# A three-block transformer kernel: compression weights in two transfers, the gate's weights in two ring slots, the first pair's sums on VectorE

## The reference, cut to what matters

```python
# first block
ssm = jax.nn.gelu(ssm)
ssm = ssm * jax.nn.sigmoid(ssm @ w_glu[l] + b_glu[l])      # w_glu: 512 x 512
x = x + _rms_norm(jnp.concatenate([attn, ssm], -1) @ w_out[l], post_norm_g[l])
# second block, for l in range(2)
parts = jnp.split(_rms_norm_2(x, g_pre_mix[l]) @ w_in[l], split_at, axis=-1)
hid = jax.nn.gelu(blocks @ w1 + b1)     # compression of keys, then of values: w1 is 2048 x 256
kc = hid @ w2 + b2                      # 31 blocks of 32 tokens, 2 heads: 62 columns
h = _rms_norm_2(x, g_pre_mlp[l])
y = jnp.square(jax.nn.relu(h @ w_up[l])) @ w_down[l]       # 1024 -> 4096 -> 1024
```

## Time and profile before

| | us |
|---|---|
| runs of the kernel before (median of 3) | 1707.92 |
| the profiled execution | 1710.8 |
| its span, first to last instruction | 1709.0 |
| TensorE busy | 1652.7 |
| VectorE, ScalarE, GpSimd busy | 1114.3, 713.3, 578.2 |

### The profile page before, as it was taken

The page is one execution under the profiler, slowest core; times in us unless marked ns, Lnnn a source line. Parts: engine busy times, 40 slices in busy tenths (PEclk is TensorE's granted clock), DMA queues, the critical chain, the costliest instruction groups (busy, mean ns, idle before and its releaser), DMA issues.

```text
span 1709.0 us, 25412 instructions
## 1 busy us (share of the span) xinstructions
PE 1652.7 (97%) x9539; PEld 1291.1 (76%) x9539; DVE 1114.3 (65%) x1955; ACT 713.3 (42%) x1426; POOL 578.2 (34%) x596
## 2 busy tenths in 40 slices
PE   7988999999999999999999999999999999999997
PEld 4455547478886668899889878887667888888886
DVE  6999756345337665777778655433774587778854
ACT  4233342252226654444444234233664454444322
POOL 1010001231205553544444724110564454444460
PEclk9999999998999999999999999899999999999999
DMA  6314230135311003333333313622000333333321
GB/s 195 68 25 93 56 123 1 28 99 165 93 50 63 2 1 99 96 102 100 99 99 99 102 37 104 184 69 99 14 2 1 99 111 100 99 99 100 100 97 49
DMA packets 195786, 137.68 MB, mean 81 GB/s; under 512 B 34871, under 2 KB 176946, under 8 KB 195666
## 3 DMA queue, kind: packets, MB, share of 16 engines
q1 hardware_dynamic: 189372, 128.86, 26.0%
q10 hardware_dynamic: 6294, 7.22, 1.8%
HBM read 131.00 MB, written 2.10 MB: 78 GB/s over the span
## 4 chain that ended last, share of the span: by engine, by line
PE 82%; DVE 9%; POOL 3%; issue 2%; DMA 2%; ACT 1%; ACTq 0%; SPq 0%; POOLq 0%; DVEq 0%
PE ps L564 14%; PE ps L565 14%; PE ps L566 14%; PE ps L2104 4%; PE ps L2105 4%; PE ps L2106 4%; PE ps L1984 4%; PE ps L2000 4%; PE ps L2015 3%; PE ps L1200 3%; PE ps L894 3%; PE ps L1879 1%; POOL U_LO L2700 1%; DMA WR<-in_cmp_w_v 1%; PE ps L1108 1%
## 5 line engine op out<-in xcount | busy, mean ns | idle before, releaser
L566 PE MATMUL ps<-HT_R,WR_R 128*128 128x512 f32 (+1 forms) x832 | 313.6, 377 | 0.0
L566 PEld LDWEIGHTS ps<-HT_R,WR_R 128*128 128x128 f32 x832 | 157.4, 189 | 32.1
L564 PE MATMUL ps<-HT_R,UP_HI 128*128 128x512 f32 x448 | 177.3, 396 | 0.0
L565 PE MATMUL ps<-HL_MLP,UP_HI 128*128 128x512 f32 x448 | 177.0, 395 | 0.0
L486 DVE TENSOR_TENSOR WR_R<-WR,UP_HI 128x1024 fp32r<-128x1024 f32 x56 | 99.9, 1785 | 103.2 <-ACT UP_HI L480 103.2
L2174 ACT ACTIVATE BIG<-ps 64x512 f32<-64x512 f32 (+3 forms) x124 | 71.7, 579 | 173.0 <-PE ps L566 153.4
L2502 DVE CUSTOM_DVE_ANT_0 ps<-ps,tri 128x512 f32<-128x512 f32 (+1 forms) x192 | 93.1, 503 | 57.8 <-PE ps L1984 57.1
L2674 POOL TENSOR_SCALAR BIG<-BIG,rg,gate 128x512 f32<-128x512 f32 (+3 forms) x128 | 76.3, 607 | 152.1 <-DVE rg L2518 151.8
L2274 ACT ACTIVATE BIG<-ps,mn 128x512 f32<-128x512 f32 (+1 forms) x192 | 100.2, 528 | 62.0 <-DVE mn L2502 54.0
L2700 POOL TENSOR_TENSOR U_LO<-BIG,U_HI 128x768 fp32r<-128x768 f32 (+1 forms) x48 | 120.5, 2531 | 1.9
L894 PE MATMUL ps<-WR,HT 128*128 128x512 f32 (+1 forms) x256 | 115.0, 600 | 1.2 <-ACT BIG L1677 1.2
(11 more groups left out here) (397 smaller groups left out, 4289.4 us busy)
## 6 DMA issues: line engine op xcount, KB each, us to landing
WR<-in_w_up SPq DMA_DIRECT2D x64, 512.0 KB, 4.0
WR<-in_w_down SPq DMA_DIRECT2D x96, 256.0 KB, 3.3
WR<-in_w_in SPq DMA_DIRECT2D x36, 512.0 KB, 5.3
WR<-in_w_out SPq DMA_DIRECT2D x6, 2048.0 KB, 7.9
WR<-in_w_in SPq DMA_DIRECT2D x5, 2048.0 KB, 8.2
WR<-in_w_down SPq DMA_DIRECT2D x16, 512.0 KB, 3.7
WR<-in_cmp_w_k SPq DMA_DIRECT2D x2, 2048.0 KB, 8.2
WR<-in_cmp_w_v SPq DMA_DIRECT2D x2, 2048.0 KB, 8.4
```

Source lines behind the costliest of these rows:

```text
L564: nc.tensor.matmul(out_, w[0], x[0], start=start, stop=False)
L565: nc.tensor.matmul(out_, w[0], x[1], start=False, stop=False)
L566: return nc.tensor.matmul(out_, w[1], x[0], start=False, stop=stop)
```

## The change

`w1v` becomes two units of two slots, `w1v0` and `w1v1`, of eight of the sixteen k blocks each; `hidden(1)` waits for the second at its ninth k. `glu` becomes a unit of two slots. The four sums of pair 0 move from GpSimd to VectorE, between `step_sums(0)` and `step_lo(0)` of each layer; the semaphore `t_sum` counts them, and `u_pool` counts one less.

```diff
-    quad("glu", [((0, 512), t_blocks(a["w_glu"][0], (0, 512)))], sem.glu_ps, T)
+    unit("glu", 2, [(None, t_blocks(a["w_glu"][0], (0, 512)))], sem.glu_ps, T)
...
-                    w1 = a[f"cmp_w1_{kind}_2"][l]
-                    unit(f"w1{kind}_{l}", 4, [(None, w1.rearrange("(k p) c -> p k c", p=P))], sem.hid_ps, 2 * l + i + 1)
+                    w1 = a[f"cmp_w1_{kind}_2"][l].rearrange("(k p) c -> p k c", p=P)
+                    if kind == "k":
+                        unit(f"w1k_{l}", 4, [(None, w1)], sem.hid_ps, 2 * l + 1)
+                        continue
+                    for part in range(2):
+                        unit(f"w1v{part}_{l}", 2, [(None, w1[:, LP // 2 * part:LP // 2 * part + LP // 2, :])], sem.hid_ps, 2 * l + 2)
...
-                wv = block_of(f"w1{'kv'[i]}_{l}", pe, CMP_HID)
+                if i == 0:
+                    wv = block_of(f"w1k_{l}", pe, CMP_HID)
+                else:
+                    slot = by_name[f"w1v0_{l}"].slot
+                    wv = WR[:, slot:slot + 4, :].rearrange("p s (k c) -> p (s k) c", c=CMP_HID)
+                    arrived(pe, f"w1v0_{l}")
                 for j in range(2):
                     for k in range(LP):
+                        if i == 1 and j == 0 and k == LP // 2:
+                            arrived(pe, f"w1v1_{l}")
...
+            def first_pair_sums():
+
+                part = lambda i: U_ALL[0][:, 256 * i:256 * i + 256]
+                dve.wait_ge(sem.u_act, N_ACT * l + 3)
+                dve_link(nc.vector.tensor_tensor(part(S1), A21_[:, 0, :], part(A22), ALU.add))
+                dve_link(nc.vector.tensor_tensor(part(S2), part(S1), part(A11), ALU.subtract))
+                nc.vector.tensor_tensor(part(S3), part(A11), A21_[:, 0, :], ALU.subtract)
+                nc.vector.tensor_tensor(part(S4), part(A12), part(S2), ALU.subtract).then_inc(sem.t_sum, 1)
...
                 step_sums(dve, l, 4 * d)
+                if d == 0:
+                    first_pair_sums()
                 step_lo(dve, l, 4 * d)
...
                 for n, cols_ in enumerate((slice(0, 768), slice(768, 1792))):
+                    if p == 0:
+                        pool.wait_ge(sem.t_sum, N_SUM * l + 2)
                     pool.wait_ge(sem.u_act, N_ACT * l + 5 * p + 4 + n)
...
-        SWAP_AT = {"w1k": (0,), "w1v": (1,), "t16": (2,), "t17": (3,), "t18": (4,), "t19": (5,)}
+        SWAP_AT = {"w1v0": (0,), "w1v1": (1,), "t16": (2,), "t17": (3,), "t18": (4,), "t19": (5,)}
```

More of the change, by code:

```diff
@@ L57 @@
 F_PLAIN = 2 * NPAIR
-N_ACT, N_POOL = 5 * NPAIR + NF - F_PLAIN, 3 * NPAIR + NF - F_PLAIN
+N_ACT, N_POOL = 5 * NPAIR + NF - F_PLAIN, 3 * NPAIR - 1 + NF - F_PLAIN
+N_SUM = NSTEP + 1
 J_LATE, J_DOWN = J_MLP + 4 + 12 * NST, J_MLP + 8 + 12 * NST
@@ L522, in step_hi @@
             nc.scalar.activation(H2[i][:], WR[:, u.slot, 512:1024], ACT.Copy).then_inc(sem.w_hi, 1)
-            act.wait_ge(sem.t_sum, NSTEP * l + n + 1)
+            act.wait_ge(sem.t_sum, N_SUM * l + (n + 2 if n else 1))
             nc.scalar.activation(WH_MLP[2 * i + 1][:], T_ALL[i], ACT.Copy).then_inc(sem.w_hi, 1)
@@ L538, in step_lo @@
             u, i = by_name[f"st{n}_{l}"], n % 2
-            dve.wait_ge(sem.t_sum, NSTEP * l + n + 1)
+            dve.wait_ge(sem.t_sum, N_SUM * l + (n + 2 if n else 1))
             dve.wait_ge(sem.w_hi, NSPLIT * l + step_number(n) + 1)
@@ L2089, in strassen_step @@
                 n, p = 4 * d + 2 * sweep + i, 2 * d + i
-                pe.wait_ge(sem.u_pool, N_POOL * l + 3 * p + 2)
+                pe.wait_ge(sem.u_pool, N_POOL * l + 3 * p + 1)
                 pe.wait_ge(sem.w_lo, NSPLIT * l + step_number(n) + 1)
@@ L2097, in strassen_step @@
                     if q == 3:
-                        pe.wait_ge(sem.u_pool, N_POOL * l + 3 * p + 3)
+                        pe.wait_ge(sem.u_pool, N_POOL * l + 3 * p + 2)
                     w = step_right(l, n, right)
@@ L2136, in two_pe @@
             for i in range(FG):
-                pe.wait_ge(sem.u_pool, N_POOL * l + 3 * NPAIR + i + 1)
+                pe.wait_ge(sem.u_pool, N_POOL * l + 3 * NPAIR + i)
                 w = down_right(i, 0)
@@ L2285, in two_act, with pair_summed @@
             mix_to_norm_act(act, w0, mixed(B1 + l), HL_MLP, lambda i: up_hi(act, l, i))
+            def pair_summed(act, p):
+                if p == 0:
+                    act.wait_ge(sem.t_sum, N_SUM * l + 2)
+                else:
+                    act.wait_ge(sem.u_pool, N_POOL * l + 3 * p)
             def unit_done(f):
@@ L2290, in unit_done @@
                 if f >= F_PLAIN + 2:
-                    act.wait_ge(sem.u_pool, N_POOL * l + 3 * NPAIR + f - F_PLAIN - 1)
+                    act.wait_ge(sem.u_pool, N_POOL * l + 3 * NPAIR + f - F_PLAIN - 2)
                 nc.scalar.activation(r, ps[UP_BANK[f]][:], ACT.Relu).then_inc(sem.u_act, 1)
@@ L2300, in unit_done @@
                 if p >= 2:
-                    act.wait_ge(sem.u_pool, N_POOL * l + 3 * (p - 2) + 1)
+                    pair_summed(act, p - 2)
                 if p >= 3:
@@ L2312, in pair_hi_sums @@
             def pair_hi_sums(p):
-                act.wait_ge(sem.u_pool, N_POOL * l + 3 * p + 1)
+                pair_summed(act, p)
                 nc.scalar.activation(U_HI[p % 3][:, 768:1792], U_ALL[p % 3][:, 768:1792], ACT.Copy).then_inc(sem.u_act, 1)
@@ L2690, in two_pool @@
             for p in range(NPAIR):
[L2691 to L2697, removed]
+                if p:
+                    part = lambda i: U_ALL[p % 3][:, 256 * i:256 * i + 256]
+                    pool.wait_ge(sem.u_act, N_ACT * l + 5 * p + 3)
+                    pool_link(nc.gpsimd.tensor_tensor(part(S1), A21_[:, p % 2, :], part(A22), ALU.add))
+                    pool_link(nc.gpsimd.tensor_tensor(part(S2), part(S1), part(A11), ALU.subtract))
+                    nc.gpsimd.tensor_tensor(part(S3), part(A11), A21_[:, p % 2, :], ALU.subtract)
+                    nc.gpsimd.tensor_tensor(part(S4), part(A12), part(S2), ALU.subtract).then_inc(sem.u_pool, 1)
+                    pool.wait_ge(sem.u_pool, N_POOL * l + 3 * p)
                 for n, cols_ in enumerate((slice(0, 768), slice(768, 1792))):
+                    if p == 0:
+                        pool.wait_ge(sem.t_sum, N_SUM * l + 2)
                     pool.wait_ge(sem.u_act, N_ACT * l + 5 * p + 4 + n)
```

## The result

The changed kernel takes 1690.08 us (median of 3 runs, 1688.80 to 1691.03) where the one before takes 1707.92: a ratio of 0.9892, 95% interval 0.9877 to 0.9908. Run again beside the single parts it had 0.9873 (0.9859 to 0.9887). The forecast was 1689.3 us, a ratio of 0.9891. Its profiled execution took 1688.8 us with a span of 1687.0; the mean granted clock is 0.993, where it was 0.983.

The account below looks back on a forecast made before the run. TensorE, busy 1652.7 of 1709.0 us, bounds the kernel. Gains of 16.2 (`w1v`) + 0 (gate's weights) + 2.4 (sums) = 18.6 us take 1707.9 to 1689.3 us; 8-in-10 range 1685.5 to 1699.

Parts of the forecast that it names:

- `w1v` in two: Compression, both layers: second half lands 3.6 us early, `hidden(1)` runs without pause at clock 1.00; 16.2 us gained.
- The cover in front of `transposed(8)`: Compression: the weights' low part is ready at 404.1, `transposed(8)` would start at 405.0; 0.9 us of cover left.
- rival B: Compression: one layer keeps its clock fall, say from a new pause before `transposed(8)`; about 1694 to 1697 us; 6%.
- the clock's: Compression: half-clock time won back, per layer 5.61 + 0.97 us in layer 0, 12.75 - 7.25 + 1.0 in layer 1.
- the likeliest case: Whole kernel: the forecast itself, 1689.3 us, held at 79%, with its own range 1686 to 1693.
- the bounds of the sums: MLP, pair 0's sums: from 4.4 us gained to 2.2 us lost; -2.0 to +4.6 about the forecast.
- The gate's weights: Gate of block 1: `glu` issued about 205, wait stays near 2.1 us; 0 us gained, bounds 0 to 1 lost.
- Rival D: Gate of block 1: the wait was for its weights; 2.1 us more gained and a clock rise, 1685 us; 2%.
- Pair 0's sums: MLP start: VectorE's sums let U_LO start 1.9 us earlier; 1.2 us gained a layer, 2.4 together.
- The walk in strict turns: MLP: VectorE and GpSimd queues alternating with bare durations; step 1 low sums end 712.8, gain 1.2 us a layer.
- A: Compression: the clock falls in `hidden(1)` all the same, leaving 3.5 us gained a layer; 1698.5 us; 9%.
- C: Compression: `w1v`'s second half comes late, over 8.8 us on the way, stopping `hidden(1)`; up to 1709.3 us; 2%.

Follow-up runs that it names:

- the part alone: The kernel before with only the gate's weights `glu` in two slots: median 1709.34 us, ratio 1.0000 (0.9992 to 1.0009).
- the copies moved: The changed kernel with VectorE copying the transposed Gelu tiles before the four low parts of the rotated queries: 1684.47 us, ratio 0.9854.
- the last pause run: The changed kernel with 512-column memset pauses before `hidden(0)` in layer 0 and between `hidden(1)` and `transposed(8)` in layer 1: median 1703.24 us.

## Why the prediction was right, step by step

*`w1v` in two.* Right in each step. The first half went out at 376.72, 0.2 us after the forget gate's transposes began, the second at 388.35, 0.2 us after `hidden(0)` began; each is 5.4 us on its way, so the second is there at 393.8, 3.4 us before its ninth k (388.11 + 7.25 + 1.8 = 397.2), for 3.6 forecast. `hidden(1)` ran at 1.00, and the pause was the cause, which the forecast could only argue. The cover in front of `transposed(8)` is 402.32 - 401.69 = 0.6 us for 0.9 forecast; rival B, which lives on it, did not come, and in the one trace with a pause of 0.70 us put there on purpose the clock stayed up.

*Its size* was met: 16.2 forecast, 16.8 between the medians and 17.7 between the means (2.6 of waits, 15.1 of clock), which the interval of about 2.7 us either way can't tell apart. The term that may be low is the clock's, 13.1. The fall that I priced from the one trace lasted 11.72 + 1.93 = 13.65 us, and so it did in both layers with only `glu` changed. With only pair 0's sums changed, where the pause is as before, it lasted 17.1 us in both layers; in layer 0, 12.47 + 4.60, with `hidden(1)` at 13.21 us:

```profile
398.83:399.57 0.74, 0.74 (x7) 1.00 0.73 139
399.57:412.04 12.47, 12.47 (x61) 0.50 0.63 159
412.04:416.64 4.60, 4.60 (x12) 0.50 0.76 247
```

That would make 1.7 us more a layer. One profiled execution can't tell how often which length occurs.

*The total*, 1690.1 us for 1689.3, is nearer than the method can promise: single executions of the changed kernel differ by up to 4.7 us (1686.3 to 1691.0), and to that extent the match is luck. The stated range of the likeliest case has a slip: the bounds of the sums and a microsecond give 1686.3 to 1694.9, not 1693.

*The gate's weights.* Right: 0, and the wait stayed at 2.08 us though `glu` was issued at 204.51 (forecast 205). It was 8.3 us on its way, not 5.2, beside `ukv` and two tables; nobody waited for it. That the wait was for VectorE's copy is now shown. Rival D had the cause wrong, but its price, the wait and a rise of the clock with it, is what this wait could cost.

*Pair 0's sums.* The walk in strict turns came out to 0.2 us nearly everywhere (10.28 added to the times after, to set them beside those of before): VectorE's sums 695.6 to 697.3 (forecast 695.7 to 697.4), U_LO of pair 0 ends 702.2 (702.2), U_LO of pair 1 711.6 (711.7), low sums of step 1 712.65 (712.8), one wait of 1.08 us (1.3). From the start of step 0 to the end of step 1 it was 12.75 us and is 706.11 - 694.74 = 11.37: 1.4 us a layer for 1.2 forecast, and 2.5 in span times clock for 2.4. The bare duration that the walk took for 1024 columns was a little low, 1.1 us for 1.22. The Trainium skill (SBUF — State Buffer, SBUF: two separate sides) says that the shared pair of ports is locked for a whole instruction; the trace agrees, with 3.43 us for an L554 that takes 1.22 when GpSimd is still, and the price with the lock (1.2 a layer) was nearer than the one without (1.9).

*The rivals.* A and B fell with the traces, D with the part alone and with the copies moved. C did not occur in any trace; how late a second half would turn the gain was not tried.

*The page's rule.* The Trainium skill (TensorE: Matmul & The Clock Gate, Why this matters for your kernels) warns of idle gaps between matmul bursts that are longer than any of these pauses. That differs from what was measured: 0.54 us of idling ahead of thin products was enough for a fall. The measurement decides.

## What to carry to other kernels

Price a short wait of TensorE by what runs behind it: ahead of thin products half a microsecond can cost 8 us; ahead of the gate's dense products 2.1 us cost itself and, in seven traces of twelve, 1.7 us of clock. In the estimate of a wait, both belong. When GpSimd and VectorE both work from SBUF, walk the two queues in turns with bare durations, and give a burst on the critical path to VectorE alone. A wait put down to "issue" is worth a look at which engine's queue holds the operation that feeds it.

## What was not expected of the hardware

- A stretch at half clock, once begun in thin products, lasts to their end however many are left (23.2 us in layer 0 of the last pause run) and 1.9 to 4.6 us into the dense ones; but 28.7 us of the same products, uninterrupted, never began one.
- A pause makes the fall likely, not certain: behind 0.75 us (layer 1) and 0.70 us (before `hidden(0)`) executions with and without it occurred, some 7 to 14 us apart; behind 0.34 us none of four had it, behind 1.5 us all 49, judged by their times.
- The short falls, 3.4 us or twice that, are not scattered at random. There are 71 of them in the 14 traces, and every one begins within a wait of TensorE of 0.5 us or more, or at most 3.2 us behind its end; such stretches are 8% of the span. The work behind them is of every kind, the gate's 512-column products too. They come back at the same few places (some 49, 75, 113 and 230 us in every kernel that has them), but which of the waits has one changes from execution to execution, and most waits of that length have none. With them the time of one kernel spreads by some 3 us either way (before: 1706.9 to 1714.0 us at a mean clock of 0.986 to 0.981). No run here was made to set them apart one by one.
